# Hybrid decoder trunk: another PSUM bank for two pieces of work in the latent-attention branch, and an index stage whose last projection chunk stands behind its last block

## The reference

```
h  = split(x @ w_in)
A  = causal attention with a decay per key            (8 heads)
B  = latent attention: q and k are expanded from a low-rank latent,
     logits = q.k (64 columns) + rotary q.k (32 columns)
C  = sparse attention over the 256 keys that an index picks:
     score = sum_h relu(iq_h . ik) * iw_h,  top 256 of each row
D  = sliding window attention with sinks
y  = concat(A*silu(gA), B*silu(gB), C*silu(gC), D*silu(gD)) @ w_out
x' = layer_norm(alpha * x + y)
```

## Time and profile before

| | |
|---|---|
| median of 3 runs | 2786.13 us (2785.22 to 2786.51) |
| profiled execution, its own time | 2783.55 us |
| span of its trace | 2781.8 us |
| granted TensorE clock, mean | 0.999 |
| PE busy | 2728.0 us (98%) |
| DVE busy | 1770.1 us (64%) |
| ACT busy | 1063.0 us (38%) |
| POOL (GpSimd) busy | 805.9 us (29%) |

### The profile page before, as it was taken

How to read it: one execution, slowest core, us unless ns; L and a number is a source line. 1 busy time by engine, 2 the same in 40 slices (tenths; PEclk the granted TensorE clock), 3 DMA queues, 4 the chain that set the end, 5 groups by cost and what they waited for, 6 DMA issues and landing times. The chain is left out here.

```text
span 2781.8 us, 41456 instructions
## 1 busy us (share of the span) xinstructions
PE 2728.0 (98%) x13882; PEld 1704.4 (61%) x13882; DVE 1770.1 (64%) x4495; ACT 1063.0 (38%) x3094; POOL 805.9 (29%) x1443
## 2 busy tenths in 40 slices
PE   8999999999999999999999999999999999999998
PEld 6446777666566677744464467776665666776443
DVE  4536777777898545465535367777788974643664
ACT  4233444344555445510032344443435553555000
POOL 1202444222233445510002033442222224555000
PEclk9999999999999999999999999999999999999999
DMA  5101111211101012142220011112111100211521
GB/s 215 47 24 48 47 47 35 67 41 62 41 19 34 24 42 82 66 153 81 102 87 15 24 48 47 47 37 70 36 63 40 34 18 26 91 36 49 186 75 46
DMA packets 92872, 163.42 MB, mean 59 GB/s; under 512 B 11696, under 2 KB 67648, under 8 KB 90872
## 3 DMA queue, kind: packets, MB, share of 16 engines
q1 hardware_dynamic: 92664, 160.77, 17.8%
HBM read 126.53 MB, written 32.08 MB: 57 GB/s over the span
## 5 line engine op out<-in xcount | busy, mean ns | idle before, releaser
L1576 PE MATMUL ps_s<-xT,w_ring 128*128 128x348 f32 (+4 forms) x1696 | 540.4, 471 | 7.5 <-DVE gate L2167 4.1
L1890 ACT ACTIVATE arena<-ps_t 16x32 f32<-16x32 f32 (+3 forms) x1048 | 368.7, 374 | 442.9 <-PE ps_t L1665 384.3
L1576 PEld LDWEIGHTS ps_s<-xT,w_ring 128*128 128x128 f32 x1696 | 313.3, 190 | 207.4 <-issue 82.8
L1877 ACT ACTIVATE arena<-arena,small 128x1040 f32<-128x1040 f32 (+8 forms) x544 | 371.9, 684 | 150.7 <-DVE small L2281 150.3
L1917 DVE MAX8 small<-score 128x8 f32<-128x1040 f32 (+5 forms) x360 | 334.0, 928 | 7.6
L2429 POOL TENSOR_SCALAR strips<-arena,small 128x16 f32<-128x16 f32 x384 | 117.2, 305 | 744.7 <-DVE small L2293 744.7
L1919 DVE MATCH_REPLACE8 score<-small,score 128x1040 f32<-128x1040 f32 (+5 forms) x360 | 328.8, 913 | 0.0
L1665 PE MATMUL ps_t<-ident,arena 128*128 128x128 f32 (+1 forms) x2016 | 301.1, 277 | 0.4 <-ACT cT L1794 0.4
L1638 PE MATMUL ps_s<-feat 64*128 64x272 f32 (+12 forms) x1680 | 295.8, 450 | 4.1 <-DVE feat L2205 2.2
L2432 POOL TENSOR_SCALAR arena<-arena,small 128x1024 f32<-128x1024 f32 (+7 forms) x384 | 290.0, 755 | 0.0
L1665 PEld LDWEIGHTS ps_t<-ident,arena 128*128 128x128 f32 (+1 forms) x2016 | 225.6, 139 | 96.0 <-issue 55.6
(11 more groups left out here) (295 smaller groups left out, 3754.1 us busy)
## 6 DMA issues: line engine op xcount, KB each, us to landing
w_ring<-in_w_feat SPq DMA_DIRECT2D x78, 512.0 KB, 3.6
mixed<-mixg SPq DMA_DIRECT2D x128, 128.0 KB, 1.7
score<-resid SPq DMA_DIRECT2D x16, 512.0 KB, 5.6
feat<-mixed SPq DMA_DIRECT2D x16, 512.0 KB, 6.5
arena<-in_w_out SPq DMA_DIRECT2D x4, 1536.0 KB, 8.0
resid<-score SPq DMA_DIRECT2D x9, 512.0 KB, 3.1
cT<-falls SPq DMA_DIRECT2D x8, 520.0 KB, 5.2
feat<-falls SPq DMA_DIRECT2D x8, 520.0 KB, 5.7
```

Of the source, the lines that this page charges most:

```text
L1576: mm = pe.matmul(ps_s[:, bank, 0:w], w_ring[:, wt % 2, k, :], xT[:, k, c0:c0 + w], start=(k == 0), stop=(k == KT - 1))
L1877: nc.scalar.activation(p, p, ACT.Exp, scale=-1.0, bias=nm[:, e:e + 1], accum_out=psums[0:M, st % 4, e:e + 1]).then_inc(S["exp_done"], 1)
L1890: a = nc.scalar.activation(dst, src, ACT.Copy)
```

## The change

Three edits in the planner; no arithmetic changes.

1. Branch B, block 8: the last piece of 512 keys goes to (O_BANK, P_BANK) and the 16-key piece to a score slot.
2. Branch B, gate tile: chunk c = 2 is summed in `free_bank()`, the first bank of the slot that block 7 takes next, in all four pairs. In pairs 1 and 2 the half chunks stand at places 0, 0, 1, 2, 3, 4, where they stood at 0, 1, 2, 3, 4, 5; place 5 is left without one. `halves()` has a new argument for it; branch C calls it without one.
3. Index stage: a block 4 never has work behind it. In the fourth pass the six chunks then stand behind blocks 8, 7, 6, 5, 3 and 2.

```
-    def halves(self, l, what, **kw):
+    def halves(self, l, what, first=None, **kw):
...
-            begun.update(self.chunk(l, wt, what, c, k1=KT // 2, **kw))
+            bank = first() if first and c == 2 else P_BANK
+            begun.update(self.chunk(l, wt, what, c, bank=bank, k1=KT // 2, **kw))
...
-                if fills[p] and (i != 4 or len(fills[p]) > 1):
+                if fills[p] and i != 4:
                     fills[p].pop(0)()
...
+        next_bank = lambda: self.free_bank()
...
         elif br == "B" and p in (1, 2):
-            for idx, work in enumerate(self.halves(l, "G", br=br, p=p)):
+            for idx, work in zip((0, 0, 1, 2, 3, 4), self.halves(l, "G", first=next_bank, br=br, p=p)):
                 put(idx, work)
+        elif br == "B":
+            for idx, work in enumerate(self.tile(l, "G", br=br, p=p)):
+                put(idx, lambda work=work, idx=idx: work(bank=None if idx else next_bank))
...
-                banks = self.slot_for(len(some), nth, P_BANK, 2 if br == "A" else 0)
+                banks = self.slot_for(len(some), nth, P_BANK, 2 if br in "AB" else 0)
```

## The result

The changed kernel takes 2796.49 us, the median of 5 runs (2795.89 to 2799.77); the kernel before took 2785.48 us in the same session (5 runs, 2785.22 to 2786.51). The ratio is 1.0039, with a 95% interval of 1.0027 to 1.0051: about 11 us slower. The forecast was +12.0 us; 2796.49 lies 1.6 us under the predicted 2798.1.

The account below looks back on a forecast made before the run. PE, busy 98% of the span, was taken as the bound, each added wait paid in full unless a later one shrinks. Terms 11.04 - 1.80 + 0 + 2.0 + 0.8 = +12.0 us on 2786.13 gave 2798.1 us, range 2790.0 to 2804.0.

Parts of the forecast that it names:

- Part 1: Branch B, block 7: its scores wait until gate chunk c = 2 is out of their bank, eight stalls, +11.04 us.
- Part 2: Branch B, pair 1, place 2: the waits of 0.74 and 1.06 us for P_BANK go, -1.80 us.
- Part 3: Branch B, block 8: its last piece in the values' bank costs nothing either way, 0 us.
- Part 4: Branch B, place 5 of pairs 1 and 2: without its half chunk, 0.5 us of wait four times, +2.0 us.
- second rival: Place 5 loses its whole cover, the wait growing to the half chunk: +19.6 us in all, 2805.7 us; chance 0.09.
- Part 5: Index stage: new waits behind block 4 and at branch A's block 8, less a ReLU wait, +0.8 us in two layers.
- first rival: Block 7's stall is covered, the gate chunk being out before PE arrives: +1.0 us in all, 2787.1 us; chance 0.10.
- third rival: DVE runs on while PE stands: block 7's stalls fall to 0.93 us, place 5 free; +6.4 us, 2792.5 us; chance 0.10.

Follow-up runs that it names:

- experiment 4: Changed kernel with the gate's line put ahead of the vector engine's top-256 steps at place 0 of branch B; 2793.95 us against 2785.73 before.
- experiment 5: Changed kernel with latent query chunks moved, one behind the gate chunk in pairs 0 to 2, place 5 covered again; 2789.49 us against 2786.70 before.
- experiment 10: Changed kernel with the gate's line ahead of the top-256 steps and latent query chunks moved behind the gate chunk; 2789.05 us against 2786.03 before.
- Experiment 3: Kernel before with only the half chunks of pairs 1 and 2 moved to places 0, 0, 1, 2, 3, 4, old banks; 2786.71 us against 2785.73.
- experiment 7: Changed kernel with the gate's first chunk left in P_BANK and the old index stage; 2822.08 us against 2786.70 before.
- experiment 8: Changed kernel with block 8's pieces in their old banks and the old index stage; 2807.21 us against 2786.70 before.

## Why the prediction came out right

**Part 1, block 7's stall: 11.04 expected, 10.5 in the brackets, 11.0 by spacing.** I worked from the starts of rows; the brackets count from a row's modelled end, which lies past the point where the next row could have started, by 0.07 us at each of the eight stalls. Compared as predicted, start to start, pair 0 of layer 0 has 748.13 - 745.85 = 2.28 us from the transposes to block 7, where it had 743.84 - 743.31 = 0.53: 1.75 us longer, 1.74 expected. Timelines of PE after, pairs 1, 2 and 3 of layer 0:

```profile
804.98 2.48 PE L1581 MATMUL ps_s<-xT,w_ring 128*128 128x344 f32 x8
809.06 1.80 PE L1643 MATMUL ps_s<-feat 64*128 64x456 f32 x8 [1.60 <-DVE gate L2172]
...
862.78 2.48 PE L1581 MATMUL ps_s<-xT,w_ring 128*128 128x344 f32 x8
866.44 1.80 PE L1643 MATMUL ps_s<-feat 64*128 64x456 f32 x8 [1.18 <-DVE gate L2172]
...
922.14 0.38 PE L1670 MATMUL ps_t<-ident,arena 128*128 128x128 f32 x2
...
923.49 1.80 PE L1643 MATMUL ps_s<-feat 64*128 64x456 f32 x8 [0.86 <-DVE gate L2172]
```

Less the 2.41 us of a half chunk pair 1 stands 4.08 - 2.41 = 1.67 us (1.58 expected) and pair 2 3.66 - 2.41 = 1.25 (1.35 expected); pair 3 stands 1.35 - 0.42 = 0.93 (0.93 expected). Layer 1 has 1.57, 1.67, 1.25 and 0.92. The sum is 11.0. That it meets the forecast so closely is partly luck: pair 1 was 0.09 us too low in each layer and pair 2 0.10 us too high. The mechanism is shown by experiments 4, 5 and 10, which shorten the stall by what each takes out of the chain or puts beside it.

**Part 2, -1.80 us: right in size, but it did not need the new bank.** The entry by L2172 at the chunk's line fell from 4.1 to 2.3 us. Experiment 3 gets the same with the old banks, so the moved half chunk is enough for it; I had given the credit to the free P_BANK. Of the new bank in pair 1 without the moved half there is no run. My working also let the vector engine catch up during the stall and had the bank free about 1 us before place 3 needs it. In the changed kernel, L2172 ends at 823.92 + 0.50 and PE starts the chunk at 825.23, so with 0.15 us for the release 0.66 us are left; in layer 1 it is 0.31 us. Experiment 3, which has no stall, leaves 0.65 and 0.32 us. The stall gave the vector engine nothing there, and the margin was a third to two thirds of what I took.

**Part 3, the piece: 0 expected, -1.0 measured.** PE did not wait for the maxima, as I had it. What I missed is the small wait for the key features at the 16-key piece, 1.9 us before and 0.9 after. Experiments 7 and 8 show what my zero rested on: each bank edit without the other costs 20 us or more, so neither has a price of its own.

**Part 4, place 5: +2.0 expected, +2.1 measured**, 0.51 us each time. The second rival, the whole half chunk lost as cover, did not happen.

**Part 5, index stage: +0.8 expected, +0.7 measured.** Behind block 4 the wait is 0.37 us, and block 8 of branch A waits 0.55 us for the key chunk, where it waited 0.54 us for the ReLU before. Timeline of PE after, answering to the earlier trace rows:

```profile
221.81 0.94 PE L1626 MATMUL ps_s<-feat 64*128 64x400 f32 x4 [0.37 <-ACT arena L1867]
...
233.68 1.35 PE L1643 MATMUL ps_s<-feat 64*128 64x16 f32 x8 [0.55 <-ACT feat L1828]
```

**The sum.** 11.0 - 1.8 - 1.0 + 2.1 + 0.7 = +11.0 us, and the stretch has +10.98. The forecast's +12.0 was 1 us too high, nearly all of it part 3. The first rival needed the gate ahead of the steps and other work behind it: experiment 10 builds that, and the stall is gone where both hold. The Trainium skill's rule on rotating banks (Perfetto Trace Analysis, Matmuls) would have made the change harmless; the trace has 8 new waits of 10.5 us, because the added bank is the one that the next group itself needs. Of the third rival, DVE using the stall to run ahead, nothing is seen: the stalls did not fall to 0.93 us, place 5 costs 0.51 us with the stall and without it, and the waits at place 2 vanish without any stall in experiment 3.

## What to carry to other kernels

A free accumulation bank is worth what stands between its last write and its next one on the matmul engine. If the next group in order needs that bank, the whole chain of the evacuation (activation, the evictor's queue, release) lies open, and what counts is the place of the eviction in the evictor's own in-order queue. Either put other matmuls behind it (here 1.3 us took 1.1 to 1.2 us off each stall) or choose a bank that is needed later, as P_BANK was in the kernel before and in experiment 3.

When two bank assignments are swapped together, price them together and each alone: here the two together cost about 10 us and each alone 20 or more. Moving one unit of work to another place also leaves a bare place, here with a wait of 0.4 to 0.5 us wherever place 3, 4 or 5 was left bare.

## What the runs showed of the hardware

A wait can cost more than its length. Stalls of 0.85 to 1.7 us never moved the granted clock in branch B. Of eight stalls of 2.78 us five were followed by work at 1.2 GHz, at a cost of 1.1 to 3.0 us each, and three by work at full clock; so it is not decided by the length of the stall alone, and what else decides it stays open here. At the start of layer 1, behind waits of 1.25 and 0.41 us with light work between them, the same fall came in five of twelve profiled executions and added 1.6 to 1.7 us. At the start of the program it came in nine of twelve, and the first index wait came 1.1 to 3.3 us later than in the other three. That alone is as large as most of the terms argued over here.
